# Two SwiGLU feed-forward layers computed with one level of Strassen's scheme

## The reference

```python
def swiglu(xn, w_gu, w_down):
    g, u = jnp.split(xn @ w_gu, 2, axis=-1)
    return (jax.nn.silu(g) * u) @ w_down

for i in range(DEPTH):
    ...
    hp = hp + swiglu(rmsnorm(hp, norm_ffn_g[i]), ffn_w_gu[i], ffn_w_down[i])
    hs = hs + swiglu(rmsnorm(hs, norm_ffn_g[i]), ffn_w_gu[i], ffn_w_down[i])
y_prompt = rmsnorm(hp, norm_final_g)
y_sample = rmsnorm(hs, norm_final_g)
```

## Time and profile before

| | |
|---|---|
| median of 3 runs | 3042.01 us (3042.0 to 3042.91) |
| the profiled execution, its own time | 3046.92 us |
| its span, first to last instruction | 3045.1 us |
| mean granted TensorE clock | 0.964 of full speed |
| busy: PE, DVE, ACT, POOL | 2757.9, 1029.9, 906.0, 1044.8 us |

### The profile page before, as it was taken

One profiled execution on the slowest core, in us unless ns is written; L12 is line 12 of the kernel. 1 busy time (PEld: TensorE's weight loads), 2 busy tenths in 40 slices (PEclk: granted clock), 3 DMA queues, 4 the chain that ended last, 5 costly groups with the idle time before them and its releaser, 6 DMA issues.

```text
span 3045.1 us, 47934 instructions
## 1 busy us (share of the span) xinstructions
PE 2757.9 (91%) x18330; PEld 2586.9 (85%) x18330; DVE 1029.9 (34%) x1742; ACT 906.0 (30%) x1521; POOL 1044.8 (34%) x528
## 2 busy tenths in 40 slices
PE   5777689999999999999998888787999999999998
PEld 4777479999999999999996666555999999999998
DVE  6899744111111111431114555443341111111114
ACT  4555454211111111322214555323232111111113
POOL 3899633122122221353315877000131221212211
PEclk8888799999999999999999999898999999999999
DMA  3111001111111111134515333898111111111112
GB/s 100 28 35 35 29 27 41 44 36 54 40 43 49 35 55 36 40 129 131 156 25 169 94 88 114 277 322 276 42 35 45 44 43 43 47 48 31 52 38 75
DMA packets 267542, 232.29 MB, mean 76 GB/s; under 512 B 20668, under 2 KB 239868, under 8 KB 267156
## 3 DMA queue, kind: packets, MB, share of 16 engines
q1 hardware_dynamic: 251639, 201.41, 21.9%
q10 hardware_dynamic: 15789, 29.36, 2.7%
HBM read 200.00 MB, written 31.58 MB: 76 GB/s over the span
## 4 chain that ended last, share of the span: by engine, by line
PE 72%; POOL 10%; issue 8%; DVE 4%; ACT 3%; DMA 2%; ACTq 0%; DVEq 0%; SPq 0%; POOLq 0%
PE PS L837 21%; PE PS L839 21%; PE PS L838 21%; POOL yp L765 7%; POOL pr L800 3%; PE PS L1182 2%; PE PS L1168 2%; DVE tm L1859 1%; PE PS L1153 1%; DMA xin<-in_x_prompt 1%; DVE hlo L1958 1%; PE PS L1154 1%; PE PS L1017 1%; ACT prods L1516 1%; DVE rs L1842 0%
## 5 line engine op out<-in xcount | busy, mean ns | idle before, releaser
L837 PE MATMUL PS<-xhi,whi 128*128 128x352 f32 x3408 | 1123.6, 330 | 117.1 <-DVE u L2011 55.0
L839 PE MATMUL PS<-xlo,whi 128*128 128x352 f32 x3408 | 1104.9, 324 | 0.0
L838 PE MATMUL PS<-xhi,wlo 128*128 128x352 f32 x3408 | 1104.4, 324 | 0.0
L725 POOL TENSOR_TENSOR wlo<-wraw,whi 128x1024 fp32r<-128x1024 f32 x178 | 426.3, 2397 | 1550.6 <-ACT whi L1353 1550.6
L837 PEld LDWEIGHTS PS<-xhi,whi 128*128 128x128 f32 x3408 | 649.0, 190 | 143.6 <-DVE u L2011 56.9
L838 PEld LDWEIGHTS PS<-xhi,wlo 128*128 128x128 f32 x3408 | 651.0, 191 | 0.0
L839 PEld LDWEIGHTS PS<-xlo,whi 128*128 128x128 f32 x3408 | 648.6, 190 | 0.0
L1953 DVE TENSOR_TENSOR ht<-PS,ht 128x352 f32<-128x352 f32 x132 | 69.1, 524 | 911.3 <-PE PS L839 908.4
L1353 ACT ACTIVATE whi<-wraw 128x1024 fp32r<-128x1024 f32 x204 | 214.5, 1052 | 541.2 <-PE PS L839 514.2
L837 PE MATMUL PS<-hhi,whi 128*128 128x352 f32 x1026 | 331.7, 323 | 8.8 <-issue 8.8
L839 PE MATMUL PS<-hlo,whi 128*128 128x352 f32 x1026 | 329.3, 321 | 0.0
(11 more groups left out here) (232 smaller groups left out, 2652.3 us busy)
## 6 DMA issues: line engine op xcount, KB each, us to landing
wraw<-in_ffn_w_gu SPq DMA_DIRECT2D x88, 512.0 KB, 3.8
kr<-in_cache_k SPq DMA_DIRECT2D x64, 512.0 KB, 8.1
vr<-in_cache_v SPq DMA_DIRECT2D x60, 512.0 KB, 8.9
wraw<-in_ffn_w_down SPq DMA_DIRECT2D x32, 384.0 KB, 3.3
wraw<-in_attn_w_in SPq DMA_DIRECT2D x24, 512.0 KB, 4.1
wraw<-in_ffn_w_down SPq DMA_DIRECT2D x32, 320.0 KB, 3.1
wraw<-in_conv_w_in SPq DMA_DIRECT2D x16, 512.0 KB, 4.1
qa<-q_hi SPq DMA_DIRECT2D x64, 128.0 KB, 3.0
```

Source lines behind the costliest of these rows:

```text
L725: nc.gpsimd.tensor_tensor(wlo[:, s, :], wraw[:, s, :], whi[:, s, :].bitcast(F32), ALU.subtract).then_inc(w_lo, 1)
L837: nc.tensor.matmul(out, wh, hi[:, k, blk(b)], start=(k == 0), stop=False)
L838: nc.tensor.matmul(out, wl, hi[:, k, blk(b)], start=False, stop=False)
L839: m = nc.tensor.matmul(out, wh, lo[:, k, blk(b)], start=False, stop=(k == kc - 1))
```

## The change

Both feed-forward layers are rewritten; all else stays, up to the counts of semaphores and the norms at their borders. The tokens are taken in two passes of 528 columns, each of which runs through all weights of the layer, and each pass is cut into two quarters of `HB` = 264 columns. One step of Strassen's scheme (in Winograd's form) is put on every 2 x 2 block product: input chunks in two halves, token quarters in two, and two output blocks: for a gate unit these are the gate block and the up block of one hidden chunk, for a down unit two output chunks. A unit then has seven products, numbered 1 to 7, in place of eight. Products 1, 2 and 4 use weights as loaded, 3, 5, 6 and 7 sums of them; the token side uses four loaded and derived tiles of x (or of the hidden features) and three more.

A pass has 38 units: 22 gate units (4 chunks of input per product, weight tiles of 128 x 512) and 16 down units in four groups of `PAIRS_OF` 2, 3, 3 and 3 pairs of hidden chunks (tiles of 128 x 256 or 128 x 384). Four down units of a group are put behind the first two gate units of the next group. The loops are gone: the order of every engine is written out.

For each unit, VectorE makes four sums of weights (`w_s`, results in `wlr`, the buffer that the low part then overwrites, and `S4`) and the low part of product 2; GpSimd makes the low parts of products 1, 3, 4, 5, 6 and 7 (`w_lo_part`); ScalarE makes all seven high parts. High and low parts `whs`, `wls` have one buffer per product, so that a part of unit N+1 waits for the product of unit N. Products 1, 6, 7 and 4 add up in one bank, which is read by ScalarE into `gt` (`read`) or added to `X` by VectorE (`add_out`) between them. VectorE combines gate and up parts, multiplies, and derives the hidden tiles (`hbr`); their high parts are ScalarE's and their low parts VectorE's.

The norm before a layer is spread over a half of the tokens at a time (`half_sum`, `half_spread`); the scaled tiles of x for the second pass (`scale_first`, `scale_second`, `x_t1` to `x_t4`, `x_low`) are made during the last down units of the first. The sums of squares for the norm behind the layer are made from `X` in the last down units of the second pass.

```diff
-    GROUPS = [6, 6, 5, 5]
+    HB = T // 4
+    HALF_T = 2 * HB
+    PAIRS_OF = [2, 3, 3, 3]
...
+        def products_in_order():
+            for N in range(4 * NU):
+                n = N % NU
+                if n == LAST_DOWN:
+                    yield from [(N - 1, 4), (N - 1, 3)] + [(N, p) for p in (1, 5, 2, 6, 7)]
+                elif n == 0:
+                    yield from [(N, p) for p in (1, 2, 6, 5, 7)]
+                else:
+                    yield from [(N, 1), (N, 2), (N - 1, 4), (N, 6), (N, 5), (N - 1, 3), (N, 7)]
+                if n == NU - 1:
+                    yield from [(N, 4), (N, 3)]
...
+            def raw_used(n):
+                sp.wait_ge(fS, 4 * n)
+                for p in (1, 2, 4):
+                    wait_low(sp, n - 1, p)
...
+            def w_lo_part(N, p):
+                pool.wait_ge(f_hi_w, HIGH[N, p])
...
+                nc.gpsimd.tensor_tensor(w_low(N, p), product_raw(N, p), w_high(N, p).bitcast(F32), ALU.subtract
+                                        ).then_inc(f_lo_p, 1)
...
+                for N in range(N0, N0 + 2 * NU):
+                    if not last_of_layer(N):
+                        w_lo_part(N + 1, 1)
+                    w_lo_part(N, 4)
+                    if not last_of_layer(N):
+                        w_lo_part(N + 1, 5)
+                    w_lo_part(N, 3)
+                    if not last_of_layer(N):
+                        w_lo_part(N + 1, 6)
+                        w_lo_part(N + 1, 7)
...
+                for k in range(w.m):
...
+                    nc.tensor.matmul(out, wh, hi, start=(k == 0 and p in (1, 2, 5)), stop=False,
+                                     skip_group_check=True)
+                    nc.tensor.matmul(out, wl, hi, start=False, stop=False, skip_group_check=True)
+                    m = nc.tensor.matmul(out, wh, lo, start=False, stop=(k == w.m - 1), skip_group_check=True)
...
+            def w_hi_part(N, p):
+                wait_slot(act, N, p)
...
+                nc.scalar.activation(w_high(N, p), product_raw(N, p), ACT.Copy).then_inc(f_hi_w, 1)
...
+                        if w.gated:
+                            read(N, 1)
+                        if more:
+                            w_hi_part(N + 1, 1)
+                            w_hi_part(N + 1, 2)
+                        if older and older.gated and n - 1 != LAST_DOWN:
+                            h_highs(N - 2)
+                        w_hi_part(N, 4)
+                        if w.gated:
+                            read(N, 2)
+                            silu(N, 0)
+                        if more:
+                            w_hi_part(N + 1, 6)
+                            w_hi_part(N + 1, 5)
+                        w_hi_part(N, 3)
+                        if w.gated:
+                            read(N, 3)
+                        if old and old.gated:
+                            silu(N - 1, 1)
+                        if more:
+                            w_hi_part(N + 1, 7)
...
+            def w_s(N, k):
...
+                if k == 1:
+                    wait_slot(dve, N, 5)
+                    ins = nc.vector.tensor_tensor(product_raw(N, 5), raw(N, 1, 0), raw(N, 1, 1), ALU.add)
+                elif k == 2:
+                    wait_slot(dve, N, 6)
+                    dve.wait_ge(fS, 4 * N + 1)
+                    ins = nc.vector.tensor_tensor(product_raw(N, 6), product_raw(N, 5), raw(N, 0, 0), ALU.subtract)
...
+                        if w.gated:
+                            first_gate(N)
+                        else:
+                            add_out(N, 1)
+                            add_out(N, 2)
+                        if old:
+                            if old.gated:
+                                first_hidden(N - 1)
+                            else:
+                                add_out(N - 1, 4)
+                        if not w.gated:
+                            add_out(N, 6)
+                        if older and older.gated and n - 1 != LAST_DOWN:
+                            h_lows(N - 2)
+                        if not w.gated:
+                            add_out(N, 5)
+                        if more:
+                            w_s(N + 1, 1)
+                            w_s(N + 1, 2)
+                        if old:
+                            if old.gated:
+                                second_gate(N - 1)
+                            else:
+                                add_out(N - 1, 3)
+                        if more:
+                            w_lo_part(N + 1)
+                        if w.gated:
+                            second_up(N)
+                        else:
+                            add_out(N, 7)
+                        if more:
+                            w_s(N + 1, 3)
+                            w_s(N + 1, 4)
+                        if old and old.gated:
+                            second_hidden(N - 1)
```

More of the change, by code:

```diff
@@ L117, in hybrid_step @@
         xlo = at("xlo", [P, C, T], FR, after("xhi"))
[L119 to L124, removed]
+        H0 = after("xlo")
+        ht = at("ht", [P, NB, BW], F32, 214144)
         xin = at("xin", [P, NT, D], F32, H0)
@@ L496, in load_pairs @@
                         load_unit(s, w, row0, kc, cols(0)[s])
[L497 to L505, removed]
+                with sp.Fori(1 if first else 0, n) as i:
                     for s in range(2):
@@ new lines, in closing_pair @@
+                square(0, 2)
+                for s in range(2):
+                    act.wait_ge(mm[s], (q + 1) * NB)
+                w_hi_part(N0, 1)
+                w_hi_part(N0, 2)
+                x_high(z, 0)
+                x_high(z, 1)
+                square(1, 2)
+                x_high(z, 2)
+                x_high(z, 3)
+                half_root(layer, 1)
+                x_high(z, 4)
+                w_hi_part(N0, 6)
+                w_hi_part(N0, 5)
+                x_high(z, 6)
@@ L1435, in closing_pair, with opening_highs @@
+            def opening_highs(q, n, r):
+                act.wait_ge(fS, 8 * NU)
+                for p in (1, 2, 4):
+                    wait_low(act, 2 * NU - 1, p)
+                hi_part(q, 1)
+                hi_part(q, 0)
+                act.wait_ge(f_mul, MUL[2 * NU - 1, 3])
+                norm_hi(n, 0)
                 norm_root(r, 1)
[L1436 to L1439 removed]
@@ new lines, in scale_second, with x_tile @@
+            def scale_second(z, row):
+                for k in range(C // 2):
+                    c = k + C // 2
+                    half = slice(token_cols(z * NU, 0).start, token_cols(z * NU, 1).stop)
+                    nc.vector.scalar_tensor_tensor(
+                        xbr[:, 2:4, k, :], X[:, c, half].rearrange("p (e t) -> p e t", t=HB),
+                        par[:, c, row:row + 1], PS[:, 6:8, 0:HB], ALU.mult, ALU.mult).then_inc(x_raw, 1)
+            def x_tile(t):
+                return xbr[:, t, :, :]
@@ new lines, in h_lows, with square_sums @@
+            def h_lows(N):
+                if unit_at(N).member == 0:
+                    h_low(N, (0, 1), 1)
+                    h_low(N, (1, 2), 2)
+                else:
+                    h_low(N, (2, 5), 3)
+                    h_low(N, (5, 7), 4)
+            def square_sums(layer, items):
+                for i in items:
+                    half = i // 8
+                    dve.wait_ge(s_sq, SQUARES[layer] + i + 1)
+                    if i % 8:
+                        dve.wait_ge(s_ssq, SQUARES[layer] + i)
+                    flat = ssq[:, :, :].rearrange("p b t -> p (b t)")[:, half * HALF_T:(half + 1) * HALF_T]
+                    nc.vector.tensor_tensor(flat, flat, sqx[:, i % 2, :], ALU.add).then_inc(s_ssq, 1)
```

842 lines of the change are left out of this document (671 added, 171 removed).

## The result

The changed kernel takes 3420.15 us (median of 4 runs, 3414.5 to 3424.2) against 3042.46 for the kernel before on the same chip: 1.124 times as long, with a 95% interval of 1.122 to 1.126. It is slower by 378 us; the forecast was slower by 242, at 3284 us, with a range of 3085 to 3440.

A forecast was written before the change was run, and what follows sets the result against it. VectorE and GpSimd blocking each other over SBUF, in a round of ordered waits, were to pace the feed-forward layers: 4 x 445 + 50 = 1830 us for 1588, +242 on 3042.0, 3284 us. Range 3085 to 3440, its own 3165 to 3400.

The forecast's parts named there:

- Sign and mechanism: Feed-forward layers: slower by 242 us, as VectorE operations with two SBUF inputs and GpSimd's SBUF reads block each other.
- TensorE's price: Feed-forward matmuls: 264 columns cost 0.123 us each, 342 us for a pass, 1367 us for all.
- The gate unit: In a pass, 14 gate units at 14.0 us and 8 beside down units at some 10.9: 283 us.
- The round as I listed it: One gate unit's chain: sums, ScalarE's high parts, GpSimd's low parts 5, 3, 6, 7, 1, 4, VectorE's remainder: 14.0 us.
- 455, "took 445": One feed-forward pass: units and waits sum to 455 us, less 10 where low part 4 or 1 falls under ScalarE's time.
- down units of three pairs: In a pass, 12 such units at 10.3 us on average, 8.8 in the steady state: 124 us.
- the borders: Starts and ends of the feed-forward layers: 20 us per layer at the start, 5 at the end, together 50.
- Shared resource: What VectorE and GpSimd use in turn: 11.8 to 12.2 us a gate unit, 374 to 388 a pass, over TensorE's 342.
- VectorE and GpSimd both busy over 75%: Sign expected in a feed-forward window of the changed profile, with TensorE busy 75%.
- TensorE paces: Rival: blocking in the feed-forward layers mostly hidden, 342 us a pass plus 98 of stalls, 2919 us; chance 0.11.
- The clock falls: Rival: TensorE at times granted 1.2 GHz, costing about 114 us in down units and starts, 3400 us; chance 0.12.
- DMA at nothing: Reading the feed-forward weights twice costs nothing; a 512 KB block lands in 3.8 us, asked for 14 us ahead.

The follow-up runs named there:

- a_same: Changed kernel with GpSimd's low parts of the weights replaced by memsets of 64, 512 and 512 columns, equal in pace but reading no SBUF: 3183.48 us.
- experiment 6: Changed kernel with ScalarE making high part 5 of the next unit before high part 6, GpSimd's order unchanged: 3293.77 us.
- experiment 4: Changed kernel with twelve small unused matmuls added before product 6 in units 2 to 33 of each pass: 3447.06 us.

## Why the prediction was right, and where it was off

- **Sign and mechanism: right.** The collision of VectorE and GpSimd, read from one row of 2.50 us and two that go in turn, is worth 237 us by a_same, the clock's share included. Exclusion and not half speed: a row of 0.43 became 1.38 to 1.52, and VectorE's PSUM rows stayed at 0.43. The Trainium skill, SBUF — State Buffer, section Who interferes with whom, states the lock for a GpSimd instruction that reads SBUF; the runs agree, as memsets, which only write, left VectorE at 0.69.
- **TensorE's price: right.** 264 columns at 0.122 us (median of the starts), for 0.123.
- **The gate unit: mean right by luck, parts not.** The forecast had 14 at 14.0 and 8 at 10.9 in a pass, 12.9 in the mean; 12.79 was measured. But the two kinds do not stand where I put them: units of 11.2 to 15.7 us alternate among those I gave 14.0. The round as I listed it ("GpSimd's low parts 5, 3, 6, 7, 1, 4") was the wrong round. It missed a link, low part 3 to the sum for product 3 to low part 6, for which GpSimd stood 0.93 us in the round shown; it took the hidden tiles at 0.43 where they stand for 1.4; and it never went through TensorE. Yet VectorE waited for product 5 before 29 of the first layer's 76 sums S5, 79.2 us in all, and products 6 and 5, which are not in my 14.0, take 3.6 us. The units in which these two kept the full clock took 12.0 and not 12.9, those in which they did not 14.1.
- **455, "took 445": the step that failed.** I took 10 us off because a low part might fall under ScalarE's time; the passes show no such saving, and 481 was measured (1923 / 4). Against the 455: the steady gate units 12.79 for 12.9 (-2); the first two gate units and the last of a pass took 53.5 us together, not 3 x 12.9 (+15); down units of three pairs 11.3 in the steady groups for 10.3 (+8), those of two pairs 8.5 for 8 (+2); the last four down units some 60 for 41 + 16 (+3). So of the 36 us a pass, 26 are the ends of a pass and the down units and 10 the deduction (and the 10.3 was mis-added: four units of 12, 10.5, 8.8 and 8.8 make 10.0 in the mean, so that my own numbers gave 451); 4 x 36 = 144, less 7 at the borders, are the 136 us between 3284 and the measurement. 3420 lies above the forecast's own range, 3165 to 3400, and 20 us inside the wide one.
- **Shared resource 11.8 to 12.2 us a gate unit, 374 to 388 a pass.** As a bound it was plausible: with the swap alone the gate unit came to 11.73. As the pace of the changed kernel it wasn't it; experiment 6 shows that the order was.
- **VectorE and GpSimd both busy over 75%: wrong.** 68% (331.6 of 485) and 61% (294.7). A lock and a chain leave both engines idle in part; neither looks full. TensorE's 75% was 79%; of the weight sums the one for product 5 took 0.99 us for 0.69 but the one for product 3 its own 0.69; and the waits for `wls` came as foretold, but before product 6 in the main and not before `whs`.
- **Rivals.** "TensorE paces", 2919 us, had the stalls too low: 98 us, where the kernels in which gate units do run at TensorE's pace show 1632 and 1723 us of feed-forward layers, 270 and 361 above the floor. With the right stalls that rival would have ended on the slower side as well. "The clock falls", 3400 us, came nearest to the measured time, and in part by its own mechanism: the granted clock was 0.91 to 0.93 in the passes, and low clock cost 124 us of product time. But it fell in steady gate units too, where the rival put no cost, in products 6 and 5 above all, which stand in the round; there it is some 70 us. How much of that lies in the 378, and in the 136 that the forecast missed, no run shows: experiment 4 put something else in its place.
- **DMA at nothing:** right to within some 12 us, though a block landed in 5.0 us rather than 3.8.

## What to carry to other kernels

Before giving GpSimd and VectorE elementwise work side by side, count VectorE operations with two SBUF inputs and GpSimd operations that read SBUF as one resource, and then lay out one round in queue order, through every engine that it passes, TensorE too: an engine that looks 60% busy can still set the pace. Here swapping two lines on ScalarE was worth 126 us, and moving GpSimd's part to VectorE 117 more: where the work fits on VectorE alone, try that early. A scheme that saves an eighth of the matmul columns has to earn its pipeline's ends first: four passes of 38 short units lost 184 us there, most of the 226 saved.

## What the runs showed of the hardware that I had not expected

- GpSimd's memset of 512 columns, 0.53 us, does not disturb VectorE at all: two-input operations beside a steady row of them kept 0.69 and 0.43 us.
- VectorE's rows overlap: 512 columns recorded at 0.69 us start 0.60 apart when nothing holds them. Sums of durations overstate a full VectorE by some 13%.
- TensorE's granted clock fell though its waits were short: behind waits of 1.9 to 2.7 us in units of 12.8, 27 of 76 gate units had a product 6 or 5 with matmuls 0.22 us apart rather than 0.12, 14% of all products.
